# First projections of a three-block transformer kernel: the rotary half swap moves from TensorE to ScalarE, and the first transfers are cut and ordered anew

## The chip, the cores and the metric

The kernel runs as one program on one core of a Trainium2 chip. TensorE (PE in the profile) multiplies, VectorE (DVE), ScalarE (ACT) and GpSimd (POOL) compute elementwise, and SyncE (SP) issues most of the transfers. The metric is the device time of one execution in microseconds. Three runs of the kernel before gave a median of 2835.09 us (2832.41 to 2835.9).

## The reference, cut to what matters

Three blocks follow each other on x of 512 tokens by 1024 channels, all in fp32. The change lies in the first projections of the first block alone: the normalised input times `w_in`, and the rotation of some of its columns by the tokens' positions.

```python
def rope(x, pos):
    half = x.shape[-1] // 2
    inv_freq = ROPE_THETA ** (-jnp.arange(half, dtype=jnp.float32) / half)
    ang = pos.astype(jnp.float32)[:, :, None] * inv_freq
    cos = jnp.cos(ang)[:, :, None, :]
    sin = jnp.sin(ang)[:, :, None, :]
    x1, x2 = xf[..., :half], xf[..., half:]
    return jnp.concatenate([x1 * cos - x2 * sin, x1 * sin + x2 * cos], axis=-1)

def mixer_layer(h, positions, w_in, ...):      # h = rmsnorm(x, norm_mix)
    proj = jnp.einsum('bsd,dc->bsc', h, w_in)
    qa, ka, va, qi, ki, wi, qb, kvb, gb, gate_a, gate_b = jnp.split(proj, SPLIT_POINTS, axis=-1)
    qa = rope(qa, positions)     # 8 heads of 64
    ka = rope(ka, positions)     # 64
    qi = rope(qi, positions)     # 8 heads of 32
    ki = rope(ki, positions)     # 32
    # qb: 8 heads of 64, wanted plain and rotated; k_slc and k_win: rotated, 64; the rest plain
```

After it come the two attentions of the block, its mixture of experts, and the two further blocks. None of these is touched.

## The kernel before

Features lie on the partitions, tokens on the free axis. The projections are cut into 28 groups (list `first`, lines 475 to 485), of 128 output features each or, for values and gates, of 128 tokens. Group g accumulates in PSUM bank g % 4. The order is: groups 0 to 3 qa, 4 and 5 the inputs of the compression, 6 k_slc, 7 to 10 v_slc (one for each 128 tokens), 11 ka, 12 and 13 qi, 14 to 17 va, 18 to 21 qb, 22 ki, 23 k_win, 24 to 27 v_win with the gates. Groups 0 to 3, 6, 11, 18 to 21 and 23 are rotated in widths of 64 (kinds "rope" and "both", eleven groups), 12, 13 and 22 in widths of 32 ("rope32").

Each engine runs its own program, in order, and waits on the others by semaphores.

- **SP** (`p1_sp`, then `cmp_sp` and `load_slabs`): the vectors, x in two transfers, the constants, the positions, five small weights, and then the weight slabs. A slab is a set of columns of `w_in` in one slot of the on-chip memory; it is loaded when the slab before it in that slot is freed. Slab sA holds the 512 columns of groups 0 to 3.
- **ACT** (`p1_act`): eight squares of x for the norm, the root, then per group g the eviction of its bank (line 556 or 558), and behind it `act_hi`, which rounds the weights of a later group to the high part of a split pair (line 295). After group 2 it computes the sines (line 437).
- **DVE** (`p1_dve`): the sum of the squares (line 355), h (line 587), the low part of h (line 592), the angles of the 64-wide groups (lines 413 to 430), and then for each g the low part of the weights of group g + 3 (`dve_lo`, line 303) followed by `rope(g)`: three operations, lines 607, 611 and 613. The first of them multiplies the swapped halves with the sine.
- **PE** (`p1_pe`): group 0 as plain fp32 products (line 648), a split group as 24 products of rounded operands (lines 317 to 319, eight times high*high, low*high, high*low), value groups plain (line 650). After the products of group g it does `swap(g - 1)`: a product (line 325, through `products`) of the evicted group with a constant 128x128 matrix `swap64` or `swap32` that exchanges the two halves of each head with a sign, into bank 5 + r % 3, where r counts the rotated groups. An fp32 product stands in the profile as two instructions.

The split pairs of the weights are two (`wp0`, `wp1`): the pair of group g is rewritten for group g + 2. So ACT can round the weights of group g + 2 only when PE has done group g, and it does so behind the eviction of group g; DVE then makes the low part, and PE wants it when group g + 1 ends.

Between group 10 and group 11 PE does the taps of the compression (lines 685 and 686), between 11 and 12 eight small products.

## Time and profile before

| | us |
|---|---|
| median of 3 runs | 2835.09 |
| lowest, highest | 2832.41, 2835.9 |
| the profiled execution | 2828.44 |
| its span (first to last instruction) | 2826.4 |
| PE busy in the span | 2662.1 |
| DVE busy | 1517.4 |
| ACT busy | 988.6 |

The profiled execution is one run by itself, and its time is the span and 2.04 us around it. It was 6.65 us under the median of the three timed runs. The page gives busy time for each engine, the span in 40 slices with the granted clock of TensorE (1.0 is 2.4 GHz, 0.5 is 1.2 GHz), the transfers, and the costliest groups of instructions. The first projections are the first 173 us of 2826, some 6 percent of it, so nearly all that is read here comes from the timeline of that stretch.

### The profile page before, as it was taken

How to read it: one execution, taken by the hardware profiler on the slowest of the kernel's cores; microseconds unless marked ns; L12 is line 12 of the kernel's file. 1: busy time of each engine (PE TensorE's matmuls, PEld its weight loads, DVE VectorE, ACT ScalarE, POOL GpSimd, SP SyncE). 2: the span in 40 equal slices, each digit the busy share in tenths (PEclk: the TensorE clock that was granted, in tenths of full speed). 3: DMA queues.
4: the chain of work that ended last, by engine and by line, in shares of the span. 5: the costliest groups of instructions: out<-in, count | busy, mean ns of one | idle time of the engine just before them, and what ended most of it. 6: DMA issues, size and time to landing. Idle time of an engine off the chain costs nothing.

```text
span 2826.4 us, 30173 instructions
## 1 busy us (share of the span) xinstructions
PE 2662.1 (94%) x12198; PEld 1986.2 (70%) x12198; DVE 1517.4 (54%) x2830; ACT 988.6 (35%) x1700; POOL 15.3 (1%) x20
## 2 busy tenths in 40 slices
PE   7989999979997999989999999979989999999998
PEld 5867677633445566668778888758778878778786
DVE  5347655457765398965344544556543233344534
ACT  3234445321213232224233332245744244432222
POOL 0000000000000000000000000000000000000000
PEclk9889999989998999999999999989999999999999
DMA  4311001299973210212213222122212432213120
GB/s 152 81 44 48 31 31 60 91 398 393 413 319 95 79 28 25 90 60 82 98 61 119 90 90 90 46 75 72 77 60 82 108 79 78 87 60 112 68 90 30
DMA packets 178750, 296.02 MB, mean 105 GB/s; under 512 B 26160, under 2 KB 120752, under 8 KB 170416
## 3 DMA queue, kind: packets, MB, share of 16 engines
q1 hardware_dynamic: 175088, 282.52, 28.6%
q0 software_dynamic: 2304, 8.39, 0.8%
q10 hardware_dynamic: 1216, 3.15, 0.3%
q8 instruction: 98, 1.61, 0.2%
q14 instruction: 44, 0.36, 0.0%
HBM read 288.79 MB, written 4.19 MB: 104 GB/s over the span
## 4 chain that ended last, share of the span: by engine, by line
PE 60%; DVE 6%; ACT 3%; issue 1%; DVEq 0%; ACTq 0%
PE ps L317 16%; PE ps L319 16%; PE ps L318 16%; PE ps L325 6%; PE ps L2007 2%; PE ps L331 1%; DVE ps L1932 1%; PE ps L340 1%; PE ps L2104 1%; PE ps L2034 0%; PE ps L384 0%; DVE x L2270 0%; DVE arena L2267 0%; DVE t L355 0%; ACT L2710 0%
## 5 line engine op out<-in xcount | busy, mean ns | idle before, releaser
L303 DVE TENSOR_TENSOR ws0l<-w,ws0h 128x1024 fp32r<-128x1024 f32 (+1 forms) x125 | 135.8, 1087 | 134.1 <-ACT ws0h L295 132.2
L303 DVE TENSOR_TENSOR ws1l<-w,ws1h 128x1024 fp32r<-128x1024 f32 (+2 forms) x125 | 134.9, 1080 | 131.2 <-ACT ws1h L295 131.1
L295 ACT ACTIVATE ws1h<-w 128x1024 fp32r<-128x1024 f32 (+2 forms) x125 | 117.3, 938 | 147.6 <-PE ps L319 142.0
L303 DVE TENSOR_TENSOR ws2l<-w,ws2h 128x1024 fp32r<-128x1024 f32 (+1 forms) x93 | 104.7, 1126 | 99.1 <-ACT ws2h L295 99.0
L295 ACT ACTIVATE ws0h<-w 128x1024 fp32r<-128x1024 f32 (+1 forms) x125 | 117.9, 943 | 103.8 <-PE ps L319 103.8
L1932 DVE SCALAR_TENSOR_TENSOR ps<-arena,ps 128x512 f32<-128x512 f32 x224 | 150.9, 749 | 0.0
L325 PE MATMUL ps<-arena 128*128 128x512 f32 (+11 forms) x440 | 134.7, 482 | 1.6 <-ACT t L752 1.1
L317 PE MATMUL ps<-hpc_hi,ws1h 128*128 128x512 f32 x320 | 128.1, 400 | 6.1 <-DVE ws1l L303 4.0
L317 PE MATMUL ps<-hpc_hi,ws2h 128*128 128x512 f32 x328 | 130.8, 399 | 1.5 <-issue 1.5
L319 PE MATMUL ps<-hpc_hi,ws2l 128*128 128x512 f32 x328 | 128.8, 393 | 0.0
L318 PE MATMUL ps<-hpc_lo,ws2h 128*128 128x512 f32 x328 | 128.8, 393 | 0.0
L317 PE MATMUL ps<-hpc_hi,ws0h 128*128 128x512 f32 x312 | 123.5, 396 | 3.3 <-ACT hpc_hi L1171 2.3
L340 PE MATMUL ps<-con,t 128*128 128x128 f32 (+1 forms) x556 | 104.2, 285 | 22.7 <-DVE t L1047 6.0
L319 PE MATMUL ps<-hpc_hi,ws1l 128*128 128x512 f32 x320 | 125.2, 391 | 0.0
L318 PE MATMUL ps<-hpc_lo,ws1h 128*128 128x512 f32 x320 | 125.2, 391 | 0.0
L1604 PE MATMUL ps<-w,arena 128*64 128x512 f32 x512 | 123.3, 615 | 0.8 <-ACT arena L1664 0.8
L319 PE MATMUL ps<-hpc_hi,ws0l 128*128 128x512 f32 x312 | 121.6, 390 | 0.0
L318 PE MATMUL ps<-hpc_lo,ws0h 128*128 128x512 f32 x312 | 121.4, 389 | 0.0
L340 PEld LDWEIGHTS ps<-con,t 128*128 128x128 f32 (+1 forms) x556 | 67.8, 141 | 72.7 <-issue 21.7
L295 ACT ACTIVATE ws2h<-w 128x1024 fp32r<-128x1024 f32 (+1 forms) x93 | 90.5, 973 | 79.5 <-PE ps L319 79.5
L325 PE MATMUL ps<-arena,t 128*128 128x64 f32 (+2 forms) x680 | 102.6, 282 | 4.9 <-ACT t L752 3.9
L325 PEld LDWEIGHTS ps<-arena,t 128*128 128x128 f32 x680 | 90.5, 194 | 20.5 <-issue 10.7
(564 smaller groups left out, 6182.3 us busy)
## 6 DMA issues: line engine op xcount, KB each, us to landing
w<-in_w_gate_up SPq DMA_DIRECT2D x32, 2048.0 KB, 12.3
w<-in_w_in SPq DMA_DIRECT2D x37, 1024.0 KB, 5.4
w<-in_w_down SPq DMA_DIRECT2D x32, 1024.0 KB, 12.7
w<-in_w_ff SPq DMA_DIRECT2D x16, 2048.0 KB, 8.2
w<-in_w_in SPq DMA_DIRECT2D x13, 2048.0 KB, 8.3
w<-in_w_in SPq DMA_DIRECT2D x48, 512.0 KB, 5.2
w<-in_w_branch SPq DMA_DIRECT2D x6, 2048.0 KB, 7.8
w<-in_w_out SPq DMA_DIRECT2D x4, 2048.0 KB, 7.6
```

Source lines behind the costliest of these rows:

```text
L295: A_(e).activation(pair_of(t)[0], tiles[t][1], ACT.Copy).then_inc(*e.inc(hi, ("hi", t)))
L303: e.go.tensor_tensor(p[1], tiles[t][1], p[0].bitcast(F32), ALU.subtract).then_inc(*e.inc(lo, ("lo", t)))
L317: e.go.matmul(bank, p[0][:, k, :], high, start=k == 0, stop=False)
L318: e.go.matmul(bank, p[0][:, k, :], low, start=False, stop=False)
L319: i = e.go.matmul(bank, p[1][:, k, :], high, start=False, stop=k == K - 1)
L325: i = e.go.matmul(bank, lt, rt, start=j == 0, stop=j == n - 1)
L331: i = e.go.matmul(dst, lt, rt, start=True, stop=True)
L340: i = e.go.transpose(dst, src, ident[0:k, 0:k])
L1604: i = e.go.matmul(bank[h_, :], rows[:, h_], weights[r], start=start, stop=stop)
L1932: i = e.go.scalar_tensor_tensor(out=cv[:, m, :] if k == 30 else b, in0=u, scalar=cw[:, m, k:k + 1], in1=b, op0=ALU.mult, op1=ALU.add)
L2007: i = e.go.matmul(ps[5][:], p[w_ // 2][:, k, :], hpN[w_ % 2][:, k, :], start=r == 0, stop=r == 23)
L2104: r = e.go.matmul(b[:, P * j:P * j + P], s[:, P * j:P * j + P], dg[t % 2], start=True, stop=True)
```

## The change

Four edits, all in the first projections:

1. x comes in four transfers of two chunks (512 KB each) and not in two of four; they are first on the queue. Then come the first 256 columns of the constants (the identity and the ones), the vectors, and only behind the first weights the rest of the constants and the positions.
2. Slab sA is two slabs of 256 columns, in slots 4 and 5, which lie in the memory of slot 0; slab sT in slot 0 now waits for both.
3. For a 64-wide group, ACT writes the swapped halves itself, straight from the group's bank into bank 5 + r % 3, in four copies of 32 partitions by 512, each with its sign. The product with `swap64` is gone from PE. The 32-wide groups keep theirs.
4. The first sines follow group 1 and not group 2.

```diff
-        sA, wA = columns(0, w1, [(0, 512)])
+        sA, wA = zip(*[columns(4 + j, w1, [(256 * j, 256)]) for j in range(2)])
...
-        slabs[sA].freed = (lo, ("lo", split_t[3]))
+        slabs[sA[0]].freed = (mm, ("tile", split_t[1]))
+        slabs[sA[1]].freed = (lo, ("lo", split_t[3]))
+        slabs[sT].also += [slabs[j].freed for j in sA]
...
         def p1_sp(e):
-            e.go.dma_start(vec[:], a["vecs"]).then_inc(*e.inc(in_con, "vec", 16))
-            for j in range(2):
-                e.go.dma_start(x[:, 4 * j:4 * j + 4, :], a["xT"][512 * j:512 * j + 512, :].rearrange("(k p) n -> p k n", p=P)
+
+            for j in range(4):
+                e.go.dma_start(x[:, 2 * j:2 * j + 2, :], a["xT"][256 * j:256 * j + 256, :].rearrange("(k p) n -> p k n", p=P)
                                ).then_inc(*e.inc(in_x[j], "x", 16))
-            e.go.dma_start(con[:], a["consts"]).then_inc(*e.inc(in_con, "con", 16))
+            e.go.dma_start(con[:, 0:256], a["consts"][:, 0:256]).then_inc(*e.inc(in_con, None, 16))
+            e.go.dma_start(vec[:], a["vecs"]).then_inc(*e.inc(in_con, "con", 16))
+            load_slabs(e, sA[1] + 1)
+            e.go.dma_start(con[:, 256:NCONST], a["consts"][:, 256:NCONST]).then_inc(*e.inc(in_rest, "con", 16))
...
-                elif g < 4 or kind == "both":
-
-                    e.go.activation(dst, b[:, 0:n], ACT.Copy, scale=-0.125).then_inc(*e.inc(ev, ("p1", g)))
+                elif kind in ("rope", "both"):
+
+                    f = -0.125 if g < 4 or kind == "both" else 1.0
+                    r = nth[g]
+                    e.go.activation(dst, b[:], ACT.Copy, scale=f).then_inc(*e.inc(own_a))
+                    e.wait_ge(*dv(("sw", r - 3) if r >= 3 else ("h1", 7)))
+                    for q in range(4):
+                        to, of = 32 * q, 32 * (q ^ 1)
+                        e.go.activation(ps[5 + r % 3][to:to + 32, :], b[of:of + 32, :], ACT.Copy, scale=f if q % 2 else -f
+                                        ).then_inc(*e.inc(ev if q == 3 else own_a, ("p1", g) if q == 3 else None))
...
-                if g == 2:
+                if g == 1:
                     act_sines(e, "a1", 0)
...
-                e.wait_ge(*mm(("sw", r)))
+                e.wait_ge(*(mm(("sw", r)) if narrow else ev(("p1", g))))
...
-                products(e, ps[5 + r % 3][:], [(sw32 if first[g][5] == "rope32" else sw64, raw_of(g))], ("sw", r))
+                products(e, ps[5 + r % 3][:], [(sw32, raw_of(g))], ("sw", r))
...
-                if g - 1 in nth:
+                if g and first[g - 1][5] == "rope32":
                     swap(g - 1)
```

SP, from its first instruction. `w_49` and `w_52` are slots 0 and 3, which hold slabs sA and sD; `arena` rows are the small weights. Before:

```order
L521 DMA vec<-in_vecs 128x125
L523 DMA x<-in_xT 128x4x512 x2
L525 DMA con<-in_consts 128x1530
L527 DMA t<-in_positions 128x512
L671 DMA arena<-in_w_k 128x64
L672 DMA arena<-in_w_k 128x64
L673 DMA arena<-in_w_v 128x64
L674 DMA arena<-in_pe_kT 128x16
L675 DMA arena<-in_pe_vT 128x16
L3130 DMA w_49<-in_w_in 128x8x512
L3130 DMA w_52<-in_w_in 128x8x512
```

Now, with the two halves of sA in `w_53` and `w_54` (slots 4 and 5):

```order
L525 DMA x<-in_xT 128x2x512 x4
L527 DMA con<-in_consts 128x256
L528 DMA vec<-in_vecs 128x125
L3140 DMA w_53<-in_w_in 128x8x256
L3140 DMA w_54<-in_w_in 128x8x256
L530 DMA con<-in_consts 128x1274
L532 DMA t<-in_positions 128x512
L681 DMA arena<-in_w_k 128x64
L682 DMA arena<-in_w_k 128x64
L683 DMA arena<-in_w_v 128x64
L684 DMA arena<-in_pe_kT 128x16
L685 DMA arena<-in_pe_vT 128x16
```

x goes first, and the weights of groups 0 to 3 pass the rest of the constants, the positions and the small weights; slab sD follows as the thirteenth row.

ACT, from the evictions of groups 0 and 1 on (`t<-ps` evicts, `wp0h` and `wp1h` are high parts of weights, `tabs<-tabs` the sines). Before:

```order
L556 ACTIVATE t<-ps 128x512 x2
L295 ACTIVATE wp0h<-w_49 128x1024
L556 ACTIVATE t<-ps 128x512
L295 ACTIVATE wp1h<-w_52 128x1024
L437 ACT_TABLE_LOAD
L437 ACTIVATE tabs<-tabs 128x512 x2
L556 ACTIVATE t<-ps 128x512
L295 ACTIVATE wp0h<-w_52 128x1024
```

Now:

```order
L563 ACTIVATE t<-ps 128x512
L567 ACTIVATE ps<-ps 32x512 x4
L295 ACTIVATE wp0h<-w_54 128x1024
L437 ACT_TABLE_LOAD
L437 ACTIVATE tabs<-tabs 128x512 x2
L563 ACTIVATE t<-ps 128x512
L567 ACTIVATE ps<-ps 32x512 x4
L295 ACTIVATE wp1h<-w_52 128x1024
L563 ACTIVATE t<-ps 128x512
L567 ACTIVATE ps<-ps 32x512 x4
L295 ACTIVATE wp0h<-w_52 128x1024
```

Four copies of 32 partitions stand between each eviction of a 64-wide group and the next high part, and the sines stand ahead of the eviction of group 2. The first of these rows is group 1's.

PE, at the end of group 4 and the start of group 5 (`ps0` and `ps1` are their banks). Before:

```order
L318 MATMUL ps0<-hpa_lo_78,wp1h_81 128x512
L319 MATMUL ps0<-hpa_hi_77,wp1l_82 128x512
L325 MATMUL ps5<-t3,con 128x512
L317 MATMUL ps1<-hpa_hi_77,wp0h_79 128x512
L318 MATMUL ps1<-hpa_lo_78,wp0h_79 128x512
```

Now:

```order
L318 MATMUL ps0<-hpa_lo_78,wp1h_81 128x512
L319 MATMUL ps0<-hpa_hi_77,wp1l_82 128x512
L317 MATMUL ps1<-hpa_hi_77,wp0h_79 128x512
L318 MATMUL ps1<-hpa_lo_78,wp0h_79 128x512
```

The product that swaps group 3 (`t3` times the constants) is gone from between the two groups; nothing takes its place on PE. It is the same at ten other places.

## Rows read from the trace of the kernel before

**Rows 1.** the page of the kernel before, busy time per engine

```profile
PE 2662.1 (94%) x12198; PEld 1986.2 (70%) x12198; DVE 1517.4 (54%) x2830; ACT 988.6 (35%) x1700; POOL 15.3 (1%) x20
```

**Rows 2.** timeline, first 9 us: start, duration, engine, line, out<-in, count, idle before

```profile
1.20 0.97 SPq L523 DMA_DIRECT2D x<-in_xT  x2
...
7.00 1.67 ACT L349 ACTIVATE t<-x 128x512 f32<-128x512 f32 x3 [4.96 <-DMA x<-in_xT]
...
8.26 5.47 DVE L355 TENSOR_TENSOR t<-t 128x512 f32<-128x512 f32 x7 [7.38 <-ACT t L349]
```

**Rows 3.** tile x in the first 30 us

```profile
DMA to landing us min/median/max: 5.8/6.9/8.0
```

**Rows 4.** transfers of the first 22 us: count, KB each, us from issue to landing

```profile
vec<-in_vecs SPq DMA_DIRECT2D x1, 62.5 KB, 1.8
```

**Rows 5.** timeline from 18 us, the first projection starts

```profile
18.39 5.36 DVE L587 SCALAR_TENSOR_TENSOR h<-x,vec,ps 128x512 f32<-128x512 f32 x8 [2.17 <-PE ps L331]
...
19.90 2.08 PE L648 MATMUL ps<-h,w 128*128 128x512 f32 x2 [1.55 <-DMA w<-in_w_in]
```

**Rows 6.** windows: stretch, us, busy PE, PEld, DVE, ACT, POOL, clock, DMA, GB/s

```profile
18.39:40.54 22.15, 20.64 (x67) 13.31 (x68) 21.63 (x34) 8.31 (x13) 0.00 (x0) 1.00 0.23 84
```

**Rows 7.** timeline of DVE, 39 to 47 us

```profile
39.32 1.23 DVE L303 TENSOR_TENSOR wp0l<-w,wp0h 128x1024 fp32r<-128x1024 f32 x1
44.66 0.69 DVE L607 TENSOR_TENSOR t<-ps,tabs 128x512 f32<-128x512 f32 x1 [4.11 <-ACT tabs L437]
...
46.59 1.22 DVE L303 TENSOR_TENSOR wp1l<-w,wp1h 128x1024 fp32r<-128x1024 f32 x1
```

**Rows 8.** timeline of PE, 40 to 54 us

```profile
40.88 0.80 PE L317 MATMUL ps<-hpa_hi,wp0h 128*128 128x512 f32 x1
...
46.74 1.02 PE L325 MATMUL ps<-t,con 128*128 128x512 f32 x2
47.86 0.50 PE L317 MATMUL ps<-hpa_hi,wp1h 128*128 128x512 f32 x1
...
53.42 1.02 PE L325 MATMUL ps<-t,con 128*128 128x512 f32 x2
```

**Rows 9.** timeline of ACT, 131 to 151 us

```profile
131.57 0.60 ACT L556 ACTIVATE arena<-ps 128x512 f32<-128x512 f32 x1 [5.29 <-PE ps L319]
...
137.02 0.60 ACT L556 ACTIVATE arena<-ps 128x512 f32<-128x512 f32 x1 [3.90 <-PE ps L319]
...
143.35 0.60 ACT L556 ACTIVATE arena<-ps 128x512 f32<-128x512 f32 x1 [4.78 <-PE ps L319]
...
149.68 0.60 ACT L556 ACTIVATE arena<-ps 128x512 f32<-128x512 f32 x1 [4.78 <-PE ps L319]
150.17 1.05 ACT L295 ACTIVATE wp0h<-w 128x1024 fp32r<-128x1024 f32 x1
```

**Rows 10.** timeline of DVE and PE beside them, 149 to 152 us

```profile
149.48 1.02 PE L325 MATMUL ps<-arena,con 128*128 128x512 f32 x2
...
151.25 1.23 DVE L303 TENSOR_TENSOR wp0l<-w,wp0h 128x1024 fp32r<-128x1024 f32 x1 [3.17 <-ACT wp0h L295]
```

**Rows 11.** line 325, 25 to 170 us: ns min/median/max, first and last start

```profile
L325 PE MATMUL ps<-t,con x20: 590/593/648, 34.1 to 165.6; 128*128 128x512 f32 x20
...
L325 PE MATMUL ps<-arena,con x8: 590/592/595, 136.8 to 156.2; 128*128 128x512 f32 x8
```

**Rows 12.** groups of ACT by form: count, busy us, mean ns, idle before

```profile
L2706 ACT ACTIVATE ps<-t 128x256 f32<-128x256 f32 x16 | 6.2, 388 | 20.9 <-DVE t L2767 20.9
...
L752 ACT ACTIVATE t<-ps 31x512 f32<-31x512 f32 x6 | 3.1, 569 | 0.0
```

**Rows 13.** windows: the half clock, and loads with 1 KB and with 2 KB pieces

```profile
78.00:101.90 23.90, 23.90 (x101) 22.64 (x100) 2.38 (x3) 5.18 (x9) 0.00 (x0) 0.50 0.38 89
142.00:147.00 5.00, 5.00 (x22) 3.78 (x21) 2.07 (x3) 1.54 (x2) 0.00 (x0) 1.00 1.07 359
16.00:18.00 2.00, 1.72 (x8) 1.73 (x8) 0.18 (x1) 0.01 (x1) 0.00 (x0) 1.00 1.06 390
```

More of the change, by code:

```diff
@@ L219, in build @@
         land = [signal(f"s_land{i}") for i in range(len(slots))]
-        in_con, in_x, in_pos = signal("s_con"), [signal("s_x0"), signal("s_x1")], signal("s_pos")
+        in_con, in_rest, in_x, in_pos = signal("s_con"), signal("s_rest"), [signal(f"s_x{j}") for j in range(4)], signal("s_pos")
         in_sw, in_z = signal("s_sw"), [signal("s_z0"), signal("s_z1")]
@@ L472, in build @@
         sE, wE = columns(3, w1, [(1960, 280), (928, 8), (896, 32), (896, 32), (896, 32), (896, 32)])
-        first = [(sA, wA, P * m, P, None, "rope", qa[:, m, :]) for m in range(4)]
+        first = [(sA[m // 2], wA[m // 2], P * (m % 2), P, None, "rope", qa[:, m, :]) for m in range(4)]
         first += [(sD, wD, 0, P, None, "copy", kcr), (sD, wD, 128, P, None, "copy", vcr)]
@@ L532, in p1_act @@
             for k in range(8):
-                e.wait_ge(*in_x[k // 4]("x"))
+                e.wait_ge(*in_x[k // 2]("x"))
                 act_square(e, n1, k, x[:, k, :])
@@ L594, in p1_dve @@
             dve_lo(e, 1)
+            e.wait_ge(*in_rest("con"))
             e.wait_ge(*in_pos(1))
@@ L630, in swap @@
                 r = nth[g]
+                e.wait_ge(*in_rest("con"))
                 e.wait_ge(*ev(("p1", g)))
@@ L633, in swap @@
                     e.wait_ge(*dv(("sw", r - 3)))
-                else:
-                    e.wait_ge(*dv(("h1", 7)))
-                products(e, ps[5 + r % 3][:], [(sw32 if first[g][5] == "rope32" else sw64, raw_of(g))], ("sw", r))
+                products(e, ps[5 + r % 3][:], [(sw32, raw_of(g))], ("sw", r))
             for g in range(NG):
@@ L657, in p1_pe @@
                     cmp_pe(e)
-            if NG - 1 in nth:
-                swap(NG - 1)
         def taps(Z, t):
```

## The prediction

> **What bounds the kernel now.** I read the page first: PE is busy for 2662.1 of 2826.4 us [rows 1], so what shortens PE's program, or lets it start sooner, should show in full. Then the timelines of the first 173 us, engine by engine. The reader is to see four things in them.
>
> Until 41 us one chain rules, and it isn't PE's. ACT's first square waits for x until 7.00, DVE then sums for 5.47 us without a gap, from 8.26 to 13.73 [rows 2]; behind a short turn through PE and ACT, DVE starts h at 18.39, and PE's first projection, which could begin with the first eighth of h, waits for its weights until 19.90 [rows 5]. From 18.39 DVE has no gap: it is busy 21.63 of the 22.15 us to 40.54 [rows 6]. The end of that is the low part of group 3's weights, begun at 39.32 [rows 7], and group 3 starts at 40.88, 1.56 us later [rows 8]. PE's own work before that fits in with little to spare, whatever its clock.
>
> From group 3 on PE rules. A group of 24 products takes 5.45 us (evictions 131.57 and 137.02, no swap between); with a swap between it takes 6.33 (143.35 and 149.68) [rows 9]. A swap costs PE 0.88 us, though its two instructions show 0.59 each [rows 11], since they overlap.
>
> Group 3 to group 4 is longer, 6.68 us (46.74 to 53.42) [rows 8]: the low part of group 4's weights starts only at 46.59, since DVE waited until 44.66 for the sines [rows 7]; 0.35 us late.
>
> Between 78.0 and 101.9 PE has the half clock, 1.2 GHz, through most of the compression's taps and group 11 [rows 13].
>
> **The head.** x's transfers are issued within 1.20 to 2.17 and land 5.8 and 8.0 us after issue, at 7.0 and about 9.7 [rows 2, 3]. So 1 MB takes some 2.7 us and the half of it 1.35. x now leaves at the head of the queue, about 0.45 us sooner, and ahead of the vectors' 0.06 MB (0.16 us). First landing: 7.0 - 1.35 - 0.6 = 5.05; the others at 6.4, 7.8 and 9.1. A square starts every 0.52 us (three in 1.67) [rows 2], so the first sum can start 1.26 us after the first landing, as now (8.26 - 7.00): 6.3. Then seven sums at 0.78; the third needs a square that is done by 7.5, the fifth by 8.9, the seventh by 10.3, and DVE comes to them at 7.9, 9.4 and 11.0. So the chain ends at 11.8 instead of 13.7: 1.9 us. Bounds: 0 if the landings are no earlier, 2.1 if DVE never waits.
>
> The weights must follow. Ahead of the first half of sA lie 2.1 + 0.2 MB, so it lands near 13, before h at 16.5; the second half, the constants and the positions follow by some 18, and they are wanted at 23 and 29. The smaller slabs have pieces of 1 KB and not 2; loads with 1 KB pieces ran at 359 GB/s and with 2 KB at 390 [rows 13], 0.2 us on a slab. Cost nothing. DVE's gapless stretch moves as it is, so group 3 starts at 40.88 - 1.9 = 39.0. **Term 1: -1.9.**
>
> The Trainium skill, page "DMA: Bandwidth & Descriptors", section on the anatomy of one DMA, speaks against the cut: about 2.0 us fixed per transfer. If these stood one behind the other, the two extra ones would cost 4 us; the two landings here, 2.7 us apart for 1 MB at the rate of the rows, leave no room for that, so they overlap.
>
> **The swaps.** Fourteen products stand on line 325 here (28 instructions) [rows 11], three of them 32-wide, which stay. Of the eleven that go, those of groups 0 and 1 stand before group 3's start, where DVE decides: worth nothing, PE waits about 2 us there instead. Nine remain (groups 2, 3, 6, 11, 18 to 21, 23), all on PE's path: 9 x 0.88 = 7.9. **Term 2: -7.9.**
>
> **The sines.** With group 3 now from 39.0 to 44.4, the sines are done when DVE's angles are (37.4 plus one sine, 38.0), ACT evicts group 2 at 38.0, copies, and rounds group 4's weights at about 40.5; DVE starts their low part at 41.6 and PE could have them by 43.1. The 0.35 us goes. **Term 3: -0.35.**
>
> **What the copies cost.** 44 copies on ACT. An eviction of the same length takes 0.60, and the next instruction starts 0.49 after it [rows 9]; 31 partitions instead of 128 take 0.57 [rows 12], so a narrow copy costs as a whole one. Call the start-to-start time c; I take 0.49, 22 us of ACT in all. They stand before the high part of the weights of group g + 2, so they lengthen this chain: end of group to eviction 0.20 (149.48 to 149.68), eviction to the next 0.49, four copies 4c, high part to low part 1.08 (150.17 to 151.25), low part to PE 1.56 (39.32 to 40.88) [rows 7 to 10]. Sum 3.33 + 4c, and PE wants it after one group, 5.45. So the copies are hidden while 4c is under 2.12, that is c under 0.53. At 0.49 the spare is 0.16 us. That is thin, and it holds in five places: behind groups 3, 18, 19, 20 and 21. Behind groups 2 and 11 there is 1 us more of room, and after group 23 no split weights follow. If copies did not overlap at all, c = 0.60, each place would lose 0.28: 1.4 us. **Term 4: 0, bounds 0 and +1.4 by these rows.** No row of before reads and writes PSUM in one ACT instruction, nor takes one quarter of the partitions to another; the nearest are a PSUM write of 256 columns at 0.388 us [rows 12], no dearer than a PSUM read of half the 0.60 and its overhead, and the 128x1024 pass at 1.05 [rows 9], which is what a copy would take if it moved its columns twice (c near 0.95). I stay with 0.49.
>
> The Trainium skill, page "ScalarE: Activation LUTs", has a price: 186 ns + 0.833 ns a column, successive ones overlapping by 93. By that c would be 0.52, term 4 still 0 with 0.04 us to spare. The same page says that ScalarE writes PSUM faster than SBUF; the trace's 0.388 us for a PSUM write at least doesn't contradict it.
>
> New waits: ACT waits for DVE's `sw` of three rotated groups back, over 10 us old by then; DVE's rope waits for the last copy, with nothing of PE's behind it. ACT's eight transfer issues after group 5 still end before group 6 does. The slab loads for ka, qb and ki start with PE's progress and land over 3 us ahead of need, also now.
>
> **Sum.** 1.9 + 7.9 + 0.35 = 10.1 us, on the profiled execution 2828.4 - 10.1 = 2818.3. That execution was 6.65 us under the median; on the median it is 2835.1 - 10.1 = **2825.0**.
>
> **Rivals.**
> - The copies cost more than the evictions, c from 0.60 to 0.90. Each tight place loses 4c - 2.12, 1.4 us in all at 0.60, 5.4 at 0.80. For it: the spare of 0.16 us is less than what a changed port could cost. Against: every ACT row follows its column count. Time 2826.4 to 2831; 12%.
> - The head gives little. The 62.5 KB of vectors land 1.8 us after their issue [rows 4], nearly all of it a transfer's own time. If x's transfers stood one behind the other with that between them, they would land every 3.15 us, the last at 5.05 + 9.45 = 14.5, and the last two squares and sums would end at 16.5, 2.8 later than now: gain 10.1 - 1.9 - 2.8 = 5.4, 2829.7. Against: the second half of x landed only 2.7 us after the first. If only the landings stay as they are: gain 8.2, 2826.9. Together 6%. The first case is also how it would go by the DMA page's fixed cost taken one by one.
> - The clock. Half clock costs half a microsecond per microsecond, and it lasts 23.9 us here [rows 13]. With other gaps in PE's program it may be some 4 us longer or shorter: 2 us, 2823 to 2827. The new 2 us wait before group 3 is a place where it could fall. 9%.
> - The other side: slower. If a copy within PSUM goes at half rate or less, ACT becomes the bound of the whole stretch: c = 1.1 loses 2.28 us in five places, 1.1 behind group 2 and 1.5 behind group 11, 14 in all, so 2839. It turns from gain to loss near c = 0.95. Nothing speaks for it but that no row shows such a copy; 3%.
>
> **How the numbers follow.** Forecast 2825 with 70% (its own range 2822 to 2828), the rivals 30%. A change of under 0.2% (5.7 us, so down to 2829.4) can't be told from none here. The forecast and the clock's case are faster nearly wholly (78%), of the copies' rival over half (7%), of the head's half (3%): 0.88 faster. Within 0.2%: 0.09. Slower: 0.03. For the range: downwards the profiled execution's own 2818.3 counts, since single executions differ by up to 7 us, upwards the two costlier cases: 2819 to 2831.
>
> **What would show it.** In the profile after: the first sum at 6.3 and the last ending at 11.8; h at 16.5; group 3 at 39.0 after about 2 us of PE idle; 5.45 us between evictions of groups 18 to 22; the copies 0.6 long and 0.49 apart; the first attention products at 163.3 instead of 173.4. It would be wrong if PE waits for `wp0l` or `wp1l` behind groups 3 and 18 to 21 (copies), if the first square is not near 5 us (head), or if the stage ends 10 us sooner and the total does not follow, which nothing here foresees.

## The result: 17 us faster, the forecast said 10

In the timed comparison the changed kernel took 2816.49 us (2814.75 to 2817.9, 4 runs) against 2833.75 (2831.55 to 2835.9) for the kernel before: ratio 0.9941 [0.9928, 0.9954], a gain of 17.3 us. It was faster, as forecast, but the time lies under the range of 2819 to 2831. A second set (e1) gave 2817.74. The profiled execution took 2815.97 us, its span is 2814.0. The 2833.75 is the median of the three runs that the forecast started from (2835.09) and a fourth, 2831.55.

The page of the changed kernel, busy time, against [rows 1]: PE has 22 instructions fewer and is busy 11.0 us less, ACT has 44 more and is busy 25.8 us more.

```profile
PE 2651.1 (94%) x12176; PEld 1979.9 (70%) x12176; DVE 1516.8 (54%) x2830; ACT 1014.4 (36%) x1744; POOL 15.3 (1%) x20
```

The head, against [rows 2] and [rows 5]. Timeline of the changed kernel (start, duration, engine, line, out<-in, count, idle before):

```profile
0.75 1.98 SPq L525 DMA_DIRECT2D x<-in_xT  x4
...
4.68 1.15 ACT L349 ACTIVATE t<-x 128x512 f32<-128x512 f32 x2 [2.65 <-DMA x<-in_xT]
...
5.94 5.47 DVE L355 TENSOR_TENSOR t<-t 128x512 f32<-128x512 f32 x7 [5.06 <-ACT t L349]
...
16.07 5.36 DVE L599 SCALAR_TENSOR_TENSOR h<-x,vec,ps 128x512 f32<-128x512 f32 x8 [2.17 <-PE ps L331]
...
37.01 1.23 DVE L303 TENSOR_TENSOR wp0l<-w,wp0h 128x1024 fp32r<-128x1024 f32 x1
38.29 0.50 PE L317 MATMUL ps<-hpa_hi,wp0h 128*128 128x512 f32 x1 [1.36 <-DVE wp0l L303]
```

The first square starts at 4.68 instead of 7.00. The seven sums have no gap in them (5.47 us, as before), so DVE never waits for x, and the whole lead arrives: h starts 2.32 us sooner, the low part of group 3's weights 2.31 sooner (39.32 to 37.01), group 3 2.6 sooner, after PE has stood idle for 1.36 us. From there PE rules, as before.

The stretch of groups 18 to 22, against [rows 9]. Timeline of ACT:

```profile
125.04 0.60 ACT L563 ACTIVATE arena<-ps 128x512 f32<-128x512 f32 x1 [5.29 <-PE ps L319]
125.67 2.33 ACT L567 ACTIVATE ps<-ps 32x512 f32<-32x512 f32 x4
127.93 1.04 ACT L295 ACTIVATE wp1h<-w 128x1024 fp32r<-128x1024 f32 x1
130.48 0.60 ACT L563 ACTIVATE arena<-ps 128x512 f32<-128x512 f32 x1 [1.51 <-PE ps L319]
...
136.13 0.60 ACT L563 ACTIVATE arena<-ps 128x512 f32<-128x512 f32 x1 [1.73 <-PE ps L319]
...
141.57 0.60 ACT L563 ACTIVATE arena<-ps 128x512 f32<-128x512 f32 x1 [1.52 <-PE ps L319]
...
147.29 0.60 ACT L570 ACTIVATE t<-ps 128x512 f32<-128x512 f32 x1 [1.79 <-PE ps L319]
```

An eviction every 5.44, 5.65, 5.44 and 5.72 us: the swaps' 0.88 us are gone, but every second group is 0.2 to 0.3 us late. One copy lasts 0.564 us (44 of them, 24.8 us), shorter than an eviction, yet four fill 2.33 us, one every (2.33 - 0.56) / 3 = 0.59, and the high part follows the eviction's start by 2.89. The links behind that are read from DVE and PE, at the start of group 20:

```profile
129.00 1.23 DVE L303 TENSOR_TENSOR wp1l<-w,wp1h 128x1024 fp32r<-128x1024 f32 x1 [11.62 <-ACT wp1h L295]
130.37 0.47 PE L317 MATMUL ps<-hpa_hi,wp1h 128*128 128x512 f32 x1
```

From the end of group 18 the chain is 0.20 + 2.89 + 1.07 + 1.37 = 5.53 us, above the group's 5.45. (The prediction had 1.56 for the last link; see term 4.) The group starts 0.1 us late and its first products follow each other a little more slowly, so the eviction behind it is 0.2 to 0.3 us late. This happens in three places (groups 5, 20 and 22), some 0.7 us in all; each loss gives the next chain its time.

The first products of the attention, the end of the stretch that the change touches:

```profile
162.94 1.18 PE L331 MATMUL ps<-arena 64*128 64x31 f32 x13 [0.72 <-ACT arena L558]
```

Before they started at 173.43: 10.5 us sooner, where the forecast had 10.1 (163.3). So the stage did what was said. The further 7 us of the timed gain lie behind it, where not an instruction was changed. The windows of the two kernels show where (stretch, us, busy PE, PEld, DVE, ACT, POOL, PE's granted clock, DMA). The kernel before: from its first attention product on for 150 us, and two parts of that:

```profile
173.43:323.43 150.00, 138.31 (x747) 100.10 (x747) 96.85 (x302) 66.44 (x198) 0.00 (x0) 0.92 0.13 37
177.00:194.10 17.10, 12.40 (x44) 9.07 (x45) 7.93 (x23) 8.01 (x22) 0.00 (x0) 0.50 0.20 61
296.50:310.10 13.60, 12.14 (x43) 7.97 (x43) 6.16 (x14) 5.87 (x13) 0.00 (x0) 0.75 0.00 1
```

The changed kernel, the group of the taps, then the same 150 us of work and the one stretch of it at half clock:

```profile
72.00:95.90 23.90, 23.90 (x102) 22.74 (x102) 4.21 (x6) 5.18 (x9) 0.00 (x0) 0.50 0.38 87
162.94:312.94 150.00, 138.32 (x758) 100.13 (x759) 98.10 (x305) 67.23 (x200) 0.00 (x0) 0.94 0.13 37
167.60:184.70 17.10, 13.50 (x47) 9.73 (x47) 7.93 (x23) 6.93 (x21) 0.00 (x0) 0.50 0.21 62
```

In the stage itself the half clock (1.2 GHz) lasts 23.9 us in both kernels. In the attention it lasts 23.9 us before (17.1 and twice 3.4) and 17.1 after. Behind the start of the attention the two profiled executions differ by 2.0 us (2655.0 and 2653.0), not by 7. But the profiled execution of before was a good one, 2828.44 against a median of 2833.75. A second profile of it (e2), at 2834.52, has 30.7 us there:

```profile
173.33:323.33 150.00, 138.31 (x731) 99.81 (x731) 96.09 (x300) 65.30 (x195) 0.00 (x0) 0.90 0.13 37
```

So the question for the experiments was: is the rest of the gain this clock, and what sets it?

### The profile page after: what moved, and what is told of

It reads as the page before. It is cut to its first block, busy times and chain, and to the rows that moved or that the text cites. A ratio compares the mean times of both kernels' runs of the same rounds, so it can differ in the third digit from the quotient of the medians.

```text
span 2814.0 us, 30178 instructions
## 1 busy us (share of the span) xinstructions
PE 2651.1 (94%) x12176; PEld 1979.9 (70%) x12176; DVE 1516.8 (54%) x2830; ACT 1014.4 (36%) x1744; POOL 15.3 (1%) x20
## 4 chain that ended last, share of the span: by engine, by line
PE 60%; DVE 6%; ACT 3%; issue 1%; DVEq 0%; ACTq 0%
PE ps L317 16%; PE ps L319 16%; PE ps L318 16%; PE ps L325 7%; PE ps L2017 2%; PE ps L331 1%; DVE ps L1942 1%; PE ps L340 1%; PE ps L2114 1%; PE ps L2044 0%; PE ps L384 0%; DVE x L2280 0%; DVE arena L2277 0%; DVE t L355 0%; ACT L2720 0%
```

## The experiments

Of every profile I took five numbers: the start of the attention (its first product, 64x31, on line 331); the end of the half-clock stretch over the taps and group 11; the time between the two, called the piece, which holds groups 12 to 27; how much half clock the 150 us from the attention's start on hold; and how much the whole execution holds from that start to its end. "Rest" is the profiled time less the start of the attention, that is all work that no edit touches. All in us.

```
kernel                     start    half clock  piece  half clock   to the   rest     median
                                    ends               in 150 us    end               timed
before, profiled           173.43   101.9       71.5   23.9         178.2    2655.0   2833.8
e2 before, copy            173.33   101.6       71.7   30.7         191.4    2661.2   2833.4
e8 before, 4 squares       174.90   102.7       72.2   30.7         191.5    2660.8   2834.3
e11 before, 5 products     174.27    99.1       75.1   30.7         185.0    2658.2   2832.5
e4 head alone              170.05    97.8       72.2   30.7         181.6    2657.7   2827.7
e12 swaps alone            169.89   101.5       68.4   30.7         170.8    2654.2   2825.6
e3 swaps and sines         163.80    96.3       67.5   17.1         157.3    2648.4   2813.0
e16 the same again         164.55    97.4       67.1   17.1         157.2    2648.6   2816.1
after, profiled            162.94    95.9       67.0   17.1         171.7    2653.0   2816.5
e1 after again             162.81    95.5       67.3   17.1         171.6    2652.7   2817.7
e5 after, 2 squares        162.57    94.3       68.3   30.7         185.2    2658.5   2820.8
e6 after, 4 squares        165.40    98.5       66.9   17.1         171.6    2653.0   2820.8
e7 after, 16 squares       171.82   104.6       67.2   17.1         172.7    2653.8   2829.3
e9 after, 4 products       166.53    98.0       68.6   30.7         185.1    2658.0   2822.5
e10 after, 8 products      165.08    94.5       70.6   17.1         171.6    2652.7   2819.1
e13 high part first        160.58    93.9       66.7   37.5         193.2    2661.2   2821.8
e14 eight copies           163.76    95.5       68.2   30.7         185.1    2658.3   2820.2
e15 late sines             167.07    99.1       68.0   23.9         178.6    2655.5   2823.0
e17 high first, 1 product  160.97    93.7       67.2   17.1         172.8    2653.9   2817.5
e18 e3 with e17's edits    165.23    97.1       68.1   23.9         178.1    2654.9   2815.8
```

Eight profiles with 17.1 us of half clock have a rest of 2652.0 us in the mean, eight with 30.7 us one of 2658.4: 6.4 us for 13.6 us of half clock, 0.47 for one. Some of that belongs to half clock further behind, which goes with it. Taken to the end of the execution the link is closer: the rest grows by 0.36 us for each microsecond of half clock, and none of the twenty lies more than 1.2 us off that line. That also holds for the small rests of e3, e16 and e12, which have 140 us of half clock behind the 150 us where most others have 154 to 156.

The timed executions say the same. Each has its mean granted clock on record: 0.9625 in the mean of the 93 executions of the kernel before that were timed beside the experiments, 0.9647 in the nine of the changed kernel. Within the 93, a clock higher by 0.001 goes with a time shorter by 2.2 us, so the difference is worth some 5 us of the 7. The remaining 2 us are not placed.

**The two kernels again, and the parts of the change (e1 to e4).** e1 and e2 are the changed kernel and the one before, unedited.

> The changed kernel once more, nothing edited. In the two traces the first projections end 10.5 us sooner, and the whole span is 12.4 us shorter; the timed medians differ by 17.3. Theory A (draws of the clock): what lies over 10.5 us is half clock in later stages, in places that change from execution to execution, and the first comparison drew it well; then five new rounds give a gain of 10.5 to 14, and the new trace has half-clock stretches at other places of the attention than the first. Theory B (systematic): the changed kernel always avoids half clock behind the first projections (the trace of before has it at 296.5 and 306.7, after has none there); then the gain is again 15 to 19 us and the new trace has none there again.

Measured: 2817.74 (2814.91 to 2821.5), ratio 0.9947 [0.9933, 0.996].

> The kernel before, nothing edited, timed against itself: what two equal kernels differ by, and a second trace of it. Both theories: 0 within 1 us. Theory A: its trace lacks one or both of the half-clock stretches at 296.5 and 306.7 or has others, and half clock in all differs from 204 us by some microseconds. Theory B: the same stretches at the same places, within 3.5 us. It also shows whether a profiled execution (2828.4 in the first) is shorter than timed ones (2833.8) as a rule.

Measured: 2833.35, ratio 0.9997 [0.9988, 1.0007]. The measurement adds nothing to the gain.

e3 is the kernel before with the swap and the sines of the change alone; e4 has the head alone (x in four transfers, two slabs). The edit of e3:

```
-                elif g < 4 or kind == "both":
+                elif kind in ("rope", "both"):
...
+                    for q in range(4):
+                        to, of = 32 * q, 32 * (q ^ 1)
+                        e.go.activation(ps[5 + r % 3][to:to + 32, :], b[of:of + 32, :], ACT.Copy, ...
...
-                if g == 2:
+                if g == 1:
                     act_sines(e, "a1", 0)
```

> Before, with the ACT copies in place of the 64-wide swap products and the sines behind group 1; transfers and slabs as before. By the prediction's terms 2 and 3, 8.25 us (2825.5); by the trace of after, with the stage's 10.5 less the head's 2.3, 8.2 us at the end of the first projections. Theory B would add up to 7 us behind them.

Measured: 2813.0 (2812.15 to 2818.3), ratio 0.9933 [0.9919, 0.9946]. The swaps and the sines bring the whole gain by themselves.

> Before, with x in four transfers, the new order of the first transfers and the two half slabs; swaps on PE and sines behind group 2, as before. By the prediction's term 1, 1.9 us; by the trace of after (h starts at 16.07 and not at 18.39) 2.3 us. Rival: the head is worth more than its 2.3 us, because something behind hangs on it: 5 us or more.

Measured: 2827.71, ratio 0.9982 [0.9973, 0.9991]: 5 to 6 us alone, and nothing on top of e3. In its profile DVE has its 2.3 us at the low part of group 3's weights (37.06), but group 3 starts only 1.8 us sooner, 39.08 and not 40.88. PE, which still does the swaps, has no gap before it:

```profile
38.62 1.02 PE L325 MATMUL ps<-t,con 128*128 128x512 f32 x2
39.08 0.80 PE L317 MATMUL ps<-hpa_hi,wp0h 128*128 128x512 f32 x1
```

The attention starts 3.4 us sooner, because the half clock over the taps was 20.5 us and not 23.9 (3.4 us less, worth 1.7); the rest is 2657.7. The 150 us of e3 and of e4 from the start of their attention, one after the other:

```profile
163.80:313.80 150.00, 138.32 (x759) 100.06 (x759) 98.06 (x305) 67.49 (x201) 0.00 (x0) 0.94 0.13 37
```

```profile
170.05:320.05 150.00, 138.32 (x731) 99.73 (x731) 96.27 (x300) 65.19 (x195) 0.00 (x0) 0.90 0.13 37
```

The clock is the eighth column: 0.94 against 0.90, so the swaps and sines together change it and the head's gain does not. (The swaps alone do not either: e12 below has 30.7 us.)

**Is it the date at which the attention starts? (e5 to e8)** If the half clock depended only on how soon all of this comes, a delay at the top would bring it back. Squares that nobody reads are put ahead of the first one, each waited for: 2, 4 and 16 in the changed kernel, 4 in the one before.

```
+                if k == 0:
+                    for _ in range(2):
+                        e.go.activation(n1.square(0)[:], x[:, 0, :], ACT.Square).then_inc(*e.inc(own_a))
+                        e.wait_ge(*e.last)
```

> The changed kernel with two further squares of x's first chunk on ACT ahead of the first one, each waited for: everything behind starts later by some 1.3 us, and nothing else is changed. Theory A (the clock's half stretches fall at random from execution to execution): 1.3 us over the changed kernel's 2817.7, so 2819. Theory C (which stretches run at half clock follows from where the program stands against its own start, so each kernel has its own): the time is off that sum by 2 us or more, up or down, and the trace has other half-clock stretches between 160 and 310 us than the two traces of the changed kernel (17.1 us in each).

> The same with four further squares, some 2.6 us later. Theory A: 2820.3. Theory C: off that sum by 2 us or more, and by another amount than with two squares.

> The same with sixteen further squares, some 10.5 us later, so that the first projections end where those of the kernel before do. Theory A: 2828.2, and the gain over before is only what the clock's draws give, 5 to 6 us. Theory C: where the stages stand as in before, they meet the same half clock, and the time comes near before's, 2830 to 2834.

> The kernel before with four further squares, 2.6 us later. Theory A: 2833.6 + 2.6 = 2836.2. Theory C: off by 2 us or more, and no slower than before at some shifts: 2830 to 2840.

Measured: 2820.77 (ratio 0.9953 [0.994, 0.9966]), 2820.82 (0.9959 [0.9946, 0.9971]), 2829.25 (0.9992 [0.9979, 1.0005]) and 2834.32 (1.0015 [1.0002, 1.0028]). e7 tells most. Its attention starts at 171.82, only 1.6 us before that of the kernel before, and still its profile has the short half clock:

```profile
171.82:321.82 150.00, 138.33 (x758) 100.20 (x759) 98.08 (x305) 67.37 (x201) 0.00 (x0) 0.94 0.13 37
```

The end of the half clock over the taps had moved with the delay (from 95.9 to 104.6), the piece stayed 67.2. e6 is like it: a start at 165.40, a piece of 66.9, 17.1 us. So the date alone does not decide. By its time e7 lies between the two theories: the median is only 3.8 us below that of the kernel before, and the interval holds 1. Ten of its twelve timed executions took 2824.3 to 2830.2 us at a granted clock of 0.964 to 0.966, two took 2842.5 and 2842.9 at 0.960.

But a delay ahead of the taps isn't always neutral. In e5 the half clock over the taps lasted 20.5 us and ended 1.6 us sooner than in the changed kernel, the piece was 68.3, and the attention, which starts 0.4 us before that of the changed kernel, has 27.3 and 3.4 us of half clock. This profiled execution took 2821.02, 5.05 longer:

```profile
166.00:193.30 27.30, 22.45 (x70) 15.32 (x71) 9.63 (x30) 10.30 (x30) 0.00 (x0) 0.50 0.13 39
220.60:224.00 3.40, 3.40 (x11) 2.60 (x10) 1.77 (x4) 1.47 (x6) 0.00 (x0) 0.50 0.02 5
```

Its five timed executions show less of it: a median of 2820.77 at a mean clock of 0.9644, against 2817.0 and 0.9647 in the nine of the changed kernel.

**Is it the length of the piece? (e9 to e11)** Products that the next one overwrites are put ahead of the swap of group 22, the last of the 32-wide ones: 4 and 8 of 256 columns in the changed kernel, 5 in the one before. (`G_Q` is 18, so the condition leaves out groups 12 and 13.)

```
+                if first[g][5] == "rope32" and g > G_Q:
+                    for _ in range(4):
+                        e.go.matmul(ps[5 + r % 3][:, 0:256], sw32, raw_of(g)[:, 0:256], start=True, stop=True)
```

> The changed kernel with four useless products of 256 columns (0.44 us each) in front of the swap of group 22, late in the first projections: PE reaches the attention 1.8 us later. Theory D: the attention's half clock depends on how long PE takes from the end of the half clock in the taps and group 11 to the start of the attention. Ten traces so far: 66.9 to 67.5 us between them go with 17.1 us of half clock in the attention (five traces), 68.3 to 72.2 us with 23.9 or 30.7 (five). The removed swaps shortened this piece by 4.5 us. Then 69 us should bring 24 to 31 us of half clock back, and the time is 1.8 + 3 to 6 us over the changed kernel: 2822 to 2825. Theory A (random draws, nothing of the change): 2819.5 and no such link.

> The same with eight such products, 3.5 us later; 70.7 us between. Theory A: 2817.7 + 3.5 = 2821.2. Theory D in its simplest form (the longer the piece, the more half clock): 70.7 us go with 24 to 31 us of it, 2824 to 2827. Theory D with a return (traces of one kernel show the clock's steps at a fixed rhythm, so a piece longer by one step of it meets the same again): 17 us of half clock, 2821 to 2822, so hardly slower than with four.

> The kernel before with five such useless products at the same place, 2.2 us more work for PE; 74 us between. Theory A: 2833.3 + 2.2 = 2835.5. Theory D simple: 30.7 us of half clock as in its own traces, 2835.5. Theory D with a return: the piece has the place of the changed kernel's again, 17 us of half clock in the attention, and the kernel is faster than before although it does more: 2829 to 2832.

Measured: 2822.53 (0.9965 [0.9954, 0.9977]), 2819.1 (0.9951 [0.9938, 0.9964]) and 2832.48 (0.9987 [0.9973, 1.0001]). e10 does twice the added work of e9 and takes 3.4 us less. Its piece is 70.6 instead of 68.6, with the short half clock again, and its stage had 20.5 instead of 27.3 us of it. Of e9 and e10:

```profile
70.70:98.00 27.30, 27.30 (x117) 26.08 (x116) 5.68 (x8) 5.18 (x9) 0.00 (x0) 0.50 0.42 91
166.53:316.53 150.00, 138.32 (x731) 99.72 (x731) 96.22 (x300) 65.21 (x195) 0.00 (x0) 0.90 0.13 37
```

```profile
165.08:315.08 150.00, 138.32 (x758) 100.19 (x759) 98.10 (x305) 67.22 (x201) 0.00 (x0) 0.94 0.13 37
```

So work behind the taps changes the attention's clock, and more of it isn't always worse. The timed executions bear this out: their mean granted clock is 0.9623 in e9 and 0.9656 in e10. The expectation of e10 had this case in it: a piece longer by some 3.5 us meets the short half clock again. e11 was to lengthen the piece of before to 74 us and into the short half clock; it got 75.1 us and 30.7, the half clock that e2 had at 71.7 and e5 at 68.3.

**The swaps alone, and the sines beside the copies (e12, e15).** e12 is e3 without the sines' move; e15 is the changed kernel with the sines put back:

```
-                if g == 1:
+                if g == 2:
                     act_sines(e, "a1", 0)
```

> Before with the ACT copies alone: transfers, slabs and the sines behind group 2 as before. By the prediction's term 2 (7.9 us) and nothing else 2825.4; with theory D's share of the clock (the same 67 us piece as the changed kernel) 2818 to 2820. Against the kernel with copies and sines (2813.0) it tells what the sines are worth: by term 3, 0.35 us; rival: 1 to 3 us, since the copies of group 2 delay the sines if they stand ahead of them.

> The changed kernel with the sines behind group 2 again: copies and head stay. The prediction gave the sines 0.35 us, from a kernel without copies. Copies alone against copies with sines differed by 12 us, of which the trace shows 2.6 of PE waiting before group 4 and 1.7 for a half-clock stretch that followed, and the rest half clock in the attention. Theory F: again 2 to 3 us of waiting before group 4 here, 2820 to 2825. Rival (the prediction's size): under 1 us, 2818.

Measured: 2825.55 (0.9971 [0.9959, 0.9982]) and 2823.03 (0.9967 [0.9954, 0.998]). By the medians e12 is 12.6 us slower than e3 (9.4 than its repetition e16), and e15 is 6.5 us slower than the changed kernel, for an edit priced at 0.35. Timeline of DVE and PE in e12:

```profile
45.98 0.69 DVE L614 TENSOR_TENSOR t<-ps,tabs 128x512 f32<-128x512 f32 x1 [5.29 <-ACT tabs L437]
...
47.92 1.22 DVE L303 TENSOR_TENSOR wp1l<-w,wp1h 128x1024 fp32r<-128x1024 f32 x1
49.28 0.47 PE L317 MATMUL ps<-hpa_hi,wp1h 128*128 128x512 f32 x1 [2.76 <-DVE wp1l L303]
```

and of ACT and PE in e15:

```profile
36.80 0.60 ACT L563 ACTIVATE t<-ps 128x512 f32<-128x512 f32 x1 [1.52 <-PE ps L319]
37.42 2.33 ACT L567 ACTIVATE ps<-ps 32x512 f32<-32x512 f32 x4
39.68 1.04 ACT L295 ACTIVATE wp1h<-w 128x1024 fp32r<-128x1024 f32 x1
40.74 1.28 ACT L437 ACT_TABLE_LOAD   x1
42.03 1.15 ACT L437 ACTIVATE tabs<-tabs 128x512 f32<-128x512 f32 x2
...
46.52 0.47 PE L317 MATMUL ps<-hpa_hi,wp1h 128*128 128x512 f32 x1 [2.51 <-DVE wp1l L303]
```

Behind the eviction of group 2 stand now the copies, the high part and only then the sines' table load. The sines end at 43.2, and DVE has its turn of the rope, three passes from 43.22 on, ahead of the low part of group 4's weights at 45.15. PE waits 2.51 us in e15 and 2.76 in e12. The stage of e15 ends 4.1 us later than that of the changed kernel, of which 1.7 is a half clock of 27.3 us instead of 23.9: over the taps it is the same, and 3.4 us more of it lie behind the wait, from 47.9 to 51.3. So beside the copies the sines' move is worth 2.5 us of PE's wait.

**Can the copies' waits be taken away? (e13, e14, e16 to e18)** e13 puts the high part ahead of the copies; e14 makes eight copies of 32x256 of the four:

```
                    e.go.activation(dst, b[:], ACT.Copy, scale=f).then_inc(*e.inc(own_a))
+                    act_hi(e, p1_ahead(g))
                     e.wait_ge(*dv(("sw", r - 3) if r >= 3 else ("h1", 7)))
```

> The changed kernel, with the high part of the next weights on ACT behind the eviction and ahead of the four copies. In the changed kernel eviction to high part takes 2.89 us (0.62 and four copies at 0.57), the weights reach PE 5.73 us after a group's end, wanted after 5.45, and PE lost 0.2 to 0.3 us in three places. Theory E (term 4 was that chain): no such wait is left, groups 18 to 22 are 5.45 us apart, the first projections end 0.7 us sooner. The time then is 2817 if the attention keeps its 17 us of half clock, and 5 us more if the 0.5 us of it that lie behind the taps move it to where 31 us are met. Rival: nothing is gained, since the late places have another cause.

> The changed kernel with each copy cut into two of 256 columns, eight for each group. The fixed part of a copy comes twice: by the rate of 0.83 ns a column seen between ACT's rows of 256 and 512 columns, 0.36 us each and 2.9 in place of 2.3 us a group. Theory E: the chain is 6.3 us, PE waits 0.9 us before groups 5, 20 and 22, and not at 21 and 23, since a wait gives the next chain its time; the first projections end 1.9 us later than in the changed kernel, and behind the taps 1.2 us of it, so the attention meets 31 us of half clock more often: 2820 to 2825. Rival: ACT has room and PE doesn't notice: 2817.7.

Measured: 2821.8 (0.9961 [0.9947, 0.9975]) and 2820.24 (0.996 [0.9948, 0.9972]). ACT of e13:

```profile
123.14 0.60 ACT L563 ACTIVATE arena<-ps 128x512 f32<-128x512 f32 x1 [5.28 <-PE ps L319]
123.63 1.05 ACT L295 ACTIVATE wp1h<-w 128x1024 fp32r<-128x1024 f32 x1
124.71 2.33 ACT L568 ACTIVATE ps<-ps 32x512 f32<-32x512 f32 x4
128.58 0.60 ACT L563 ACTIVATE arena<-ps 128x512 f32<-128x512 f32 x1 [1.54 <-PE ps L319]
...
134.02 0.60 ACT L563 ACTIVATE arena<-ps 128x512 f32<-128x512 f32 x1 [1.54 <-PE ps L319]
```

The waits are gone, 5.44 us everywhere, and the stage ends at 160.58, 2.4 us sooner (0.7 of it the waits, 1.7 a shorter half clock). That shows the copies' cost to PE in this stage to be the chain's 0.2 to 0.3 us a time. By the medians the kernel is 4 to 5 us slower for all that, though its seven executions reach from 2816.1 to 2830.24 and its interval overlaps that of the changed kernel. Its attention has the longest half clock of all, 37.5 us:

```profile
160.58:310.58 150.00, 139.02 (x720) 101.58 (x720) 94.66 (x297) 64.47 (x192) 0.00 (x0) 0.87 0.13 37
```

In e14 the eight copies take 2.55 us, one every 0.31, so cutting them makes it 0.22 dearer (ACT of e14):

```profile
131.53 2.55 ACT L568 ACTIVATE ps<-ps 32x256 f32<-32x256 f32 x8
134.01 1.04 ACT L295 ACTIVATE wp0h<-w 128x1024 fp32r<-128x1024 f32 x1
136.75 0.60 ACT L563 ACTIVATE arena<-ps 128x512 f32<-128x512 f32 x1 [1.70 <-PE ps L319]
```

Its stage ends 0.8 us later, its attention has 30.7 us of half clock.

With the last runs I repeated e3 (e16), and gave e13 the edit of e9 with one product instead of four (e17), and e3 both (e18). If e13 loses by the clock alone, a little more work behind the taps must be able to make it faster.

> Copies and sines without the head once more, on another draw of chip and executions; it was the fastest so far (2813.0 against 2817.7 of the changed kernel), though its first projections end 0.9 us later. Theory G (draws): this time it isn't faster than the changed kernel's 2816 to 2818. Theory H (its own place against the clock's steps, 20.5 and not 30.7 us of half clock between 860 and 1180 us): again 2812 to 2814, at a mean clock of 0.968.

> The changed kernel with the high part first, as in the run that gave 2821.8, plus one useless product of 256 columns (0.44 us of PE) before the swap of group 22. In that run's trace the piece from the end of the half clock to the attention was 66.7 us and the attention had 37.5 us of half clock; all traces with 66.9 to 67.5 us had 17.1. Theory D: the useless product brings it to 67.1 us, the attention to 17 us of half clock, and the kernel gets faster by it: 2813 to 2817. Theory A: 2821.8 + 0.4, 2822.

> The kernel with copies and early sines but the transfers of before (2813.0 and 2816.1 in two runs), with the same two edits. Its two traces show pieces of 67.5 and 67.1 us; the high part first takes off some 0.5 us and the product gives back 0.44. Theory D: about the same piece and clock, and 0.3 us less ahead of it: 2812 to 2816, the fastest if its 20.5 us of half clock between 860 and 1180 us come again. Theory A: the same as without the edits, 2813 to 2816; the two theories don't part here.

Measured: 2816.14 (2813.17 to 2819.06; 0.9944 [0.9931, 0.9957]), 2817.5 (2814.82 to 2819.55; 0.9943 [0.993, 0.9957]) and 2815.8 (2812.19 to 2820.17; 0.9933 [0.9919, 0.9946]). By the medians e17 is 4.3 us faster than e13 with more work on the path; its stage ends 0.4 us later than e13's, and its clock is back at 0.94:

```profile
160.97:310.97 150.00, 138.32 (x758) 100.12 (x759) 98.08 (x305) 67.28 (x201) 0.00 (x0) 0.94 0.13 37
```

The times alone don't prove it: the two intervals overlap, and two of e13's seven executions took 2816.1. The granted clock of the timed executions goes the same way, 0.9627 in the mean of e13 and 0.9646 in that of e17.

None of these versions is faster than the changed kernel by more than the runs scatter: e3 and e16 lie at 2813.0 and 2816.1, the two sets of the changed kernel at 2816.5 and 2817.7.

## Why the prediction was wrong, step by step

The forecast of 2825.0 was 8.5 us above the 2816.49: 1.3 us because the median of the kernel before came out at 2833.75 and not 2835.09, 0.4 us in the stage, and 6.8 us behind it.

- **Term 1, the head: 1.9 us, measured 2.3**, past its stated bound of 2.1. The landings were the part that was mis-sized: the first square could start at 4.68 and not 5.05, and the last sum ended at 11.4. DVE's stretch to group 3 is as long as before (22.17 us against 22.15 in [rows 6]), and PE waits 1.36 us there, of the 2 forecast. The cut didn't cost the fixed time of its transfers one by one, as the trace of before already said. The Trainium skill, page "DMA: Bandwidth & Descriptors", section "Anatomy of one DMA", gives the 2.0 us of the prediction for transfers issued by GpSimd; those of x are issued by SyncE.
- **Term 2, the swaps: 7.9 us, right, and 0.4 too small.** Only the three 32-wide swaps are left as 512-column products on line 325. The swap of group 1, priced at nothing, still ran when group 3 began: that group took 5.86 us in [rows 8] (40.88 to 46.74), not 5.45. Timeline of PE in the kernel before:

```profile
40.42 1.02 PE L325 MATMUL ps<-t,con 128*128 128x512 f32 x2
```

- **Term 3, the sines: 0.35 us, as read from the kernel before, where no run has the edit alone; wrong beside the copies.** I priced the edit against the kernel before, by itself. Beside the copies it keeps PE from a wait of 2.5 us (e15). The sum of the change was not hurt by that, only its parts.
- **Term 4, the copies: 0, measured +0.7.** Start to start they take 0.59 and not 0.49, between my value and the bound of 0.60, and PE waits in three of the five places. Two links of the chain were off as well, one each way: the first copy starts 0.62 behind the eviction and not 0.49, and the low part reaches PE in 1.37 us and not 1.56, which was read where the swap of group 1 still ran (40.42). With 1.37 in place of 1.56 the terms of the prediction would have hidden the copies up to c = 0.58. The rival "copies cost more" was right in its mechanism, and small. Its upper end of 2831 fits c = 0.80; the 0.90 that it names gives at least 7.4 us by its own formula, and 2832. The Trainium skill, page "ScalarE: Activation LUTs", section "What ACT_TABLE_LOAD costs", would give an estimate of 0.52; this row differs, and the row decides.
- **The sum for the stage: 10.1 us, measured 10.5** (2.3 + 7.9 + 0.4 + 0.35 - 0.7 = 10.25). That it came so near is in part luck: the misses of the terms, 0.4, 0.4 and -0.7, nearly cancel.
- **The step that failed is the clock's rival: "With other gaps in PE's program it may be some 4 us longer or shorter: 2 us, 2823 to 2827."** It looked at the stage, where the half clock is 23.9 us in both profiles, and took the difference as a scatter of both signs, worth 2 us. The runs showed a shift of one sign in the work behind the stage. The attention of the kernel before has 23.9 to 30.7 us of half clock in two profiles, that of the changed one 17.1 in both. By medians, less the start of the attention, the rest is 2833.75 - 173.43 = 2660.3 before and 2816.49 - 162.94 = 2653.6 after: 6.8 us, against the 6.4 that go with 13.6 us of half clock in the table, and the 5 that go with the clocks of the timed executions. The prediction itself named the case that would prove it wrong, "if the stage ends 10 us sooner and the total does not follow, which nothing here foresees"; it came about with the other sign.
- **The profiled execution.** It was 6.65 us under the median; I carried the gain over to the median as if the two differed by noise. Part of that is the same clock: e2, at 2834.52, has 6.8 us more half clock in the attention. A row for it stood in the trace (the clock from 177 to 194, and from 296 to 310), and I had read the clock only up to the stage's end.

What is shown and what isn't. Shown: the same instructions, started at another time against the half clock's end over the taps, get 17.1 to 37.5 us of half clock in the attention, and profiled executions differ by 5 to 7 us with it (e5 against e1 by 5.5, e13 against e17 by 7.0; the timed medians of these pairs by 3.0 and 4.3). Shown: a delay ahead of the taps can be carried over with the short half clock kept (e6, e7), but was not in e5, and work removed or added behind them does not stay neutral (e3 against e4, e9 against e10).

Not shown is a cause of the clock's steps, or a rule that was tested ahead over its whole range. The twenty profiles can be put in order afterwards, though. The first half-clock stretch of the attention starts 4.2 to 4.8 us behind its first product in all eight profiles with 17.1 us, 3.6 to 3.7 us behind it in the three with 23.9, 2.9 to 3.5 in the eight with 30.7, and 1.6 in e13. The pieces sort in the same way if those some 3.5 us apart are taken together: 66.9 to 67.5 and 70.6 had 17.1; 68.0 to 68.1 and 71.5 had 23.9; 68.2 to 68.6, 71.7 to 72.2 and 75.1 had 30.7; 66.7 had 37.5. In this order the change moved the attention from a place with 23.9 or 30.7 us to one with 17.1. Of the runs made to test the piece, e9 and e17 had the half clock that was expected, e10 one of the two cases named for it, and e11 missed the length it was meant for. Each profile is a single execution, and the kernel before has shown two values, at pieces of 71.5 and 71.7. What sets the further half clock behind the 150 us is open; no experiment was made there.

Whether the head is worth anything on the whole stays open as well: alone it brings 1.8 us at group 3 and 5 to 6 us in the total; on top of the swaps the stage ends 0.9 to 1.7 us sooner than in e3 and e16, and the total does not.

## What to carry to other kernels

Where PE is the bound and its clock drops in places, a saving isn't only its own time: read the granted clock through the stages behind the edit too, take its lengths from two or more profiles, and let the range reach as far as the largest of them, in both directions. Before a small improvement is kept or thrown away by its total time, look whether its stage ended sooner, and at its granted clock: e13 shortened its stage by 2.4 us and came out 4 to 5 us slower by the medians, with more half clock; with one product added the short half clock was back. Price an edit beside the other edits it comes with, not against the kernel before: the sines' move was priced at 0.35 us alone and was worth 2.5 us behind the copies.

## What the runs showed of the hardware beside this

- ScalarE copies of 32x512 from PSUM to PSUM, to other partitions, last 0.564 us each (44 of them, 561 to 568 ns), less than an eviction of 128x512 (0.60), but start 0.59 apart where an eviction and the pass into SBUF behind it start 0.49 apart. In two halves each they last 0.35 and start 0.31 apart. The first copy starts 0.62 behind the eviction.
- PE dropped to half clock while it was busy without a gap: in the kernel before it is busy for all of the 4.8 us from 73.2 to 78.0 at full clock and for 23.90 of the 23.90 us at half clock behind them; in the changed kernel the half clock is the same 23.90 of 23.90. In the attention it is busy 13.5 of 17.1 us of it. The length came in few sizes: 20.5, 23.9 or 27.3 us over the taps in every profile, whatever was edited.
- The halved first transfer of x landed 3.9 us after its issue where the whole one took 5.8, and the other three without a wait for DVE behind it.
